# Eight modulation tiles summed on VectorE in the first feed-forward part, gate rows in memory of their own, first loads in four pieces, a seventh tile buffer

## The chip, the cores and the metric

The kernel runs on one core of a Trainium2 chip. The metric is the device time of one execution in microseconds. Before the change, three runs took 2201.83, 2201.08 and 2201.52 us, a median of 2201.52.

## What is computed

Two transformer blocks on 256 tokens of width 1024, batch 1, all in float32. The first block has a mixer (gated convolution, short convolution, windowed pooling), a cross-attention to a memory of 256 tokens, and a mixture of 32 experts of which each token takes four. The second block has two layers, and this is where the change is:

```python
def ada_mod(c, w, b):                      # c: (1, 1024), w: (1024, 6144)
    m = jax.nn.silu(c) @ w + b
    return jnp.split(m[:, None, :], 6, axis=-1)

for layer in range(2):
    shift_m, scale_m, gate_m, shift_f, scale_f, gate_f = ada_mod(c, ada_w[layer], ada_b[layer])
    h = rms_norm(x, norm_gains[layer, 0]) * (1 + scale_m) + shift_m
    y = attention(h) if layer == 0 else retention(h)      # "attn_hybrid_mixer", "retention_mixer"
    x = x + gate_m * y
    h = rms_norm(x, norm_gains[layer, 1]) * (1 + scale_f) + shift_f
    x = x + gate_f * swiglu(h, ffn_w_gate_up[layer], ffn_w_down[layer])
```

The attention of layer 0 has eight heads of stick-breaking attention and eight of causal softmax attention. ada_w holds 2 x 6 x 1024 columns, which the kernel reads as 24 tiles of 1024 x 512.

## The kernel before

**Tiles and units.** All weights pass through a ring of four buffers (`RING = 4`, 2 MB each: 128 partitions, 8 chunks of rows, 512 columns). A planner (class `Plan`) numbers the tiles in the order of their loads; tile n goes to buffer (n + shift) mod 4, and SyncE issues its load in that order once tile n - 4 is freed (`load_tile`; the wait is on the counter in `freed`: finished TensorE products, or finished ada products). SyncE's queue is strictly in order, so a tile whose buffer is not free holds back all behind it.

**Products.** A tile is cut into two units. For each unit ScalarE makes a rounded copy, `w_high` (three buffers, line 1370), and VectorE writes the remainder over the tile itself, `ring_low` (line 1901). TensorE then does three matmuls for each pair of chunks (high x high, high x low, low x high): `feature` (line 753) with the weights as the stationary side, 48 matmuls a unit, or `token` (line 774) with the activations as the stationary side, 24 a unit. `high_until(n)` and `low_until(n)` are the places in ScalarE's and VectorE's program up to which units are prepared; `ahead(g)` is how far before the evacuation of group g.

**Experts.** The 32 experts (and more rounds if an expert has over 64 tokens) run in a loop with six buffers, the four of the ring for the gate-up weights (four tiles of 2 MB, `gu_tile`) and two more for the down weights (`down_tile`). TensorE frees a buffer through `m_tile`. In a round it does gate-up tiles 0 and 1, gathers the next expert's tokens (line 967), gate-up tiles 2 and 3, turns inputs, then the down product (line 1014) and the scatter (line 1039). Behind the experts, the plan's tiles N1, N1 + 1, ... go into the ring again, the first four as soon as the last experts' tiles are used; two of those buffers hold the last expert's down weights until then.

**Modulation.** `ada_product(i)` (line 821) multiplies silu(c) with one ada_w tile on TensorE, eight matmuls with 32 stationary columns, four at a time in different column groups, into a bank that gathers a set of tiles. `ada_take` (ScalarE, line 1503) copies the bank, `ada_reduce` (TensorE, line 829) adds and transposes it, and VectorE adds the bias (`ada_in`, `modulation`). The sets are tiles 0 to 11, 12 to 14, 15 to 21, 22 and 23. Products 12 and 13 stand around the first transposition behind the experts, 14 between `aq[0]` and `ak[0]`, 15 to 21 between the softmax steps of the attention, 22 and 23 at the entry of the first feed-forward part. Their tiles stand at the same places in the order of loads.

**Gates.** For x + gate * y the gate is needed as a row on all partitions: VectorE scales the identity by the gate column (`gate_diags`, line 2500), TensorE multiplies it with ones (`gate_rows`, line 799, banks 4 and 5), ScalarE copies it (`gate_row_in`, line 1465). `gate_diag` and `gate_row` lie in the part of the arena that also holds the softmax pairs, and in layer 0 the three steps stand directly before the product with att_w_o (`ao`).

**Softmax half.** For head pairs m = 0 to 3: `soft_scores` (TensorE, line 1181), `soft_mask` (VectorE, lines 2434 to 2439), `soft_exp` (ScalarE, 1737), `soft_scale` (VectorE, 2449), `soft_turn` (TensorE, 1193), `soft_turned` (ScalarE, 1746), `soft_out` (TensorE, 1109). The pairs are held in two buffers, and the steps of the four pairs interleave in an order written out by hand on each engine.

**Start.** SyncE loads xT in two halves, then the first tile in two column parts, then the parameters, then the rest. ScalarE splits x and the first units, VectorE makes the low parts; its wait for the parameters (`par_in`) stands ahead of the first low part (line 1893).

## Time and profile before

| | |
|---|---|
| median of three runs | 2201.52 us |
| the profiled execution | 2200.33 us |
| its span, first to last instruction | 2198.5 us |
| busy TensorE, weight loads | 2061.8 us (94%), 1380.7 us (63%) |
| busy VectorE, ScalarE | 1027.5 us (47%), 677.4 us (31%) |
| bytes moved | 652.76 MB, 297 GB/s on average |
| chain that ended last | TensorE 61%, DMA 32%, VectorE 4%, ScalarE 2% |

A page of the profile gives sums over the whole span; the stages differ, so the windows, the chain of waits and the timeline are read stage by stage. PE is TensorE, DVE VectorE, ACT ScalarE, SPq the queue of SyncE. The stages lie as follows in the span: start and mixer to about 360 us, cross-attention and routing to 467, experts to 1395, norm and the first transpositions to 1418, attention to 1575 with the softmax half from 1511 to 1552, first feed-forward part from 1587 to 1775, retention to 1997, second feed-forward part to the end.

### The profile page before, as it was taken

Reading aid. Unit: us, or ns where it says so; the run is one execution under the profiler, and the core shown is the slowest. Engines: PE = TensorE matmul, PEld = TensorE weight load, DVE = VectorE, ACT = ScalarE, POOL = GpSimd, SP = SyncE. Lnnn points to the kernel's source line nnn. Section 1 sums busy time; section 2 is a strip of 40 time slices with the busy share of each in tenths; the row PEclk is TensorE's granted clock in tenths of the full one; section 3 lists DMA queues with packets and bytes.
Section 4 is the critical chain, followed back from the end, with each engine's and each line's share of the span. In section 5 each row is a group of like instructions: output and inputs, shape, how many; then the busy total and the mean of one; then the engine's idle time right before and its main releaser. Section 6 shows DMA issues by size and latency. Waiting matters only on the chain.

```text
span 2198.5 us, 30034 instructions
## 1 busy us (share of the span) xinstructions
PE 2061.8 (94%) x12342; PEld 1380.7 (63%) x12342; DVE 1027.5 (47%) x1601; ACT 677.4 (31%) x868; POOL 3.0 (0%) x10
## 2 busy tenths in 40 slices
PE   7999999999999999999999999699899999999998
PEld 7999987743333333333333333485699888878996
DVE  6999857442222222222222223565555556555554
ACT  4343544421111111111111111353533443544333
POOL 0000000000000000000000000000000000000000
PEclk9999999999999999999999999899899999999999
DMA  9555669689999999999999999766845454444552
GB/s 321 183 176 180 239 227 338 233 351 428 428 429 429 427 429 429 428 429 429 428 429 429 428 429 429 289 230 225 273 154 192 172 179 166 154 154 153 175 178 80
DMA packets 182072, 652.76 MB, mean 297 GB/s; under 512 B 6720, under 2 KB 70208, under 8 KB 156896
## 3 DMA queue, kind: packets, MB, share of 16 engines
q1 hardware_dynamic: 181984, 651.47, 75.7%
q8 instruction: 69, 1.13, 0.2%
q14 instruction: 19, 0.16, 0.0%
HBM read 650.40 MB, written 1.05 MB: 296 GB/s over the span
## 4 chain that ended last, share of the span: by engine, by line
PE 61%; DMA 32%; DVE 4%; ACT 2%; issue 1%; SPq 0%; DVEq 0%; ACTq 0%
PE bank L753 31%; DMA ring<-w_down 29%; PE bank L774 13%; PE pair L1014 6%; PE bank L987 4%; DMA ring<-att_w_qkv 1%; DMA ring<-att_w_o 1%; PE pair L821 1%; DVE ring_low L1901 1%; PE bank L742 1%; PE pair L967 1%; ACT arena L1439 1%; DMA par<-params 0%; PE pair L1039 0%; ACT w_high L1370 0%
## 5 line engine op out<-in xcount | busy, mean ns | idle before, releaser
L1901 DVE TENSOR_TENSOR ring_low<-ring,w_high 128x2048 fp32r<-128x2048 f32 (+1 forms) x179 | 404.6, 2266 | 285.0 <-ACT w_high L1370 283.5
L753 PE MATMUL bank<-x_high,w_high 128*128 128x256 f32 x1760 | 502.4, 285 | 17.1 <-DVE ring_low L1893 15.0
L753 PE MATMUL bank<-x_low,w_high 128*128 128x256 f32 x1760 | 499.0, 284 | 0.0
L753 PE MATMUL bank<-x_high,ring_low 128*128 128x256 f32 x1760 | 498.9, 283 | 0.0
L987 PE MATMUL bank<-ring,arena 128*64 128x512 f32 x2048 | 457.3, 595 | 16.6 <-DMA ring<-w_gu 14.8
L1370 ACT ACTIVATE w_high<-ring 128x2048 fp32r<-128x2048 f32 (+1 forms) x179 | 337.7, 1891 | 255.6 <-PE bank L753 122.0
L753 PEld LDWEIGHTS bank<-x_high,w_high 128*128 128x128 f32 x1760 | 338.8, 192 | 21.3 <-issue 20.4
L987 PEld LDWEIGHTS bank<-ring,arena 128*64 128x64 f32 x2048 | 142.0, 137 | 321.6 <-issue 269.6
L753 PEld LDWEIGHTS bank<-x_low,w_high 128*128 128x128 f32 x1760 | 338.9, 193 | 1.1 <-issue 1.0
L2313 DVE TENSOR_TENSOR arena<-bank,par 128x512 f32<-128x512 f32 x64 | 44.0, 687 | 630.8 <-PE bank L997 630.8
L753 PEld LDWEIGHTS bank<-x_high,ring_low 128*128 128x128 f32 x1760 | 338.7, 192 | 0.0
L1014 PE MATMUL pair<-ring,arena 128*64 128x512 f32 x992 | 225.4, 598 | 41.6 <-DMA ring<-w_down 41.6
L774 PE MATMUL bank<-w_high,arena_r 128*128 128x512 f32 x672 | 210.2, 392 | 6.8 <-issue 4.9
L1014 PEld LDWEIGHTS pair<-ring,arena 128*64 128x64 f32 x992 | 67.9, 136 | 178.0 <-issue 177.9
L774 PEld LDWEIGHTS bank<-w_high,arena_r 128*128 128x128 f32 x672 | 127.0, 189 | 37.7 <-issue 8.0
L774 PE MATMUL bank<-ring_low,arena_r 128*128 128x512 f32 x336 | 131.5, 391 | 0.0
L1638 ACT ACTIVATE arena<-bank 128x512 f32<-128x512 f32 x64 | 34.7, 594 | 224.7 <-PE bank L987 224.7
L1950 DVE SCALAR_TENSOR_TENSOR arena<-a_pad,par,arena 128x256 f32<-128x256 f32 x240 | 98.4, 480 | 0.3
L1653 ACT ACTIVATE arena<-pair 128x512 f32<-128x512 f32 x31 | 18.5, 597 | 231.0 <-PE pair L1014 231.0
L1627 ACT ACTIVATE arena<-pair 128x512 f32<-128x512 f32 x32 | 19.1, 597 | 225.5 <-PE pair L967 225.5
L2331 DVE TENSOR_TENSOR arena<-arena,pair 128x512 f32<-128x512 f32 x124 | 76.7, 680 | 5.5 <-PE pair L1039 5.5
L774 PEld LDWEIGHTS bank<-ring_low,arena_r 128*128 128x128 f32 x336 | 63.4, 189 | 13.0
(325 smaller groups left out, 1774.7 us busy)
## 6 DMA issues: line engine op xcount, KB each, us to landing
ring<-w_gu SPq DMA_DIRECT2D x128, 2048.0 KB, 24.9
ring<-w_down SPq DMA_DIRECT2D x63, 2048.0 KB, 25.4
ring<-ada_w SPq DMA_DIRECT2D x24, 2048.0 KB, 11.8
ring<-ffn_w_gate_up SPq DMA_DIRECT2D x44, 1024.0 KB, 7.6
ring<-ret_w_in SPq DMA_DIRECT2D x12, 2048.0 KB, 7.8
ring<-w_in SPq DMA_DIRECT2D x10, 2048.0 KB, 8.1
ring<-w_in SPq DMA_DIRECT2D x16, 1024.0 KB, 10.7
ring<-ffn_w_down SPq DMA_DIRECT2D x8, 2048.0 KB, 7.7
```

What stands on the lines that cost most here:

```text
L742: pe.matmul(acc_bank[:, 0:T], w[:, k, 0:P], xs[:, k, :], start=k + n == 0 and arrival == "x_high", stop=k == b.kc - 1 and arrival == "x_sp ...
L753: mm = pe.matmul(acc_bank[:, ch * T:(ch + 1) * T], w[:, k, ch * P:(ch + 1) * P], xs[:, kk, :], start=kk + ch + n == 0, stop=kk == b.kc - 1 ...
L774: mm = pe.matmul(acc_bank[:, :], xs[:, kk, i * P:(i + 1) * P], w[:, k, :], start=kk + n == 0, stop=kk == b.kc - 1 and n == 2)
L821: mm = pe.matmul(ada_bank[s][o:o + 32, :], silu_c[:, at_col:at_col + 32], at(ada[i])[:, k, :], start=j == 0 and k < 4, stop=last and k >= ...
L987: mm = pe.matmul(bank[b][64 * o:64 * o + 64, :], xgT[:, k // 4, k % 4, :], gu_ring[t][:, j, D * o + 512 * b:D * o + 512 * b + 512], start= ...
L1014: mm = pe.matmul(bank[7][64 * o:64 * o + 64, :], actT[:, k, :], down_ring[t][:, j, 512 * o:512 * o + 512], start=k == 0, stop=k == DC - 1)
L1370: nc.scalar.activation(high_part(u), raw_part(u), ACT.Copy).then_inc(sem("w_high"), 1)
L1638: nc.scalar.activation(gu_s[b], bank[b][:, :], ACT.Copy).then_inc(sem("m_gus"), 1)
L1901: V.tensor_tensor(low_part(u), raw_part(u), high_part(u).bitcast(F32), ALU.subtract).then_inc(sem("w_low"), 1)
L1950: V.scalar_tensor_tensor(out=conv[:, c, :], in0=a_pad[:, c, tap:tap + T], scalar=pc("conv_a_w", tap * DC + c), in1=conv[:, c, :], op0=ALU. ...
L2313: V.tensor_tensor(tv, bank[2 + b][:, :].rearrange("p (c j) -> p c j", c=8), bias, ALU.add).then_inc(sem("m_vec"), 1)
L2331: V.tensor_tensor(acc[:, i, f], acc[:, i, f], bank[4 + q][:, :], ALU.add).then_inc(sem("m_acc"), 1)
```

## The change

- **Start.** The loads of xT and of the first column part of the first tile alternate in halves of 512 KB each; ScalarE and VectorE split them in that order, and VectorE's wait for the parameters moves behind the first low parts. ScalarE does one small activation ahead of the first data.
- **Seventh buffer.** `spare` (16 KB on each partition) takes gate-up tile 0 of expert 1, loaded behind xo[0]. TensorE reads it there in the first round, which is now written out ahead of the loop. The buffer of that tile takes expert 2's instead. The DMA scratch is cut to 512 to make room.
- **Gates.** After that, half of the same memory holds `gate_row` and `gate_diag`. The gate rows of layer 0 are made between `aq[0]` and `ak[0]`, in banks 4 and 6; those of layer 1's retention get their diagonals earlier.
- **Modulation.** The sets are tiles 0 to 11, 12 to 15, 16 to 23. Tiles 12 to 15 are loaded in twos ahead of aq[0] and ak[0] and multiplied around the first transpositions. Tiles 16 to 23 are loaded in the first feed-forward part, and VectorE sums each in eight steps (chunk times a column of silu(c), added up) into 512 columns; TensorE then adds the partitions with a column of ones, four tiles at a time (`ada_rows`). A tile's buffer is freed by its eighth step.
- **Norm.** `mean_w` goes; `ones` takes its place and 1/D moves into the instructions that read the sums.

```diff
-ADA_SETS = (range(0, 12), range(12, 15), range(15, 22), range(22, 24))
+ADA_SETS = (range(0, 12), range(12, 16), range(16, 24))
+ADA_SUMS = len(ADA_SETS[2])
+ADA_AT = (1, 3, 5, 7, 9)
+ADA_STEPS_DOWN = (4, 0, 4, 4, 0, 0)
...
+        spare = sb("spare", [P, 2, 2 * D])
...
+                if i < ADA_SETS[2].start:
+                    t.freed = [("ada_product", i + 1)]
+                else:
+                    t.freed = [("ada_sum", DC * (i - ADA_SETS[2].start + 1))]
...
-        ada_tiles(1)
+        ada_tiles(2)
         aq.append(plan.block([(qkv_w, 0, 512)]))
-        ada_tiles(1)
+        ada_tiles(2)
         ak.append(plan.block([(qkv_w, D, 512)]))
-        ada_tiles(1)
...
-        ada_tiles(len(ADA_SETS[2]))
-        ada_group = plan_groups(1)[0]
         b_outs = plan_groups(2)
         ao = [plan.block([(a["att_w_o_2"][0], 512 * i, 512)], token=True) for i in range(2)]
-        ada_tiles(len(ADA_SETS[3]))
...
             for i in range(FC // 2):
+                if layer == 0 and i in ADA_AT:
+                    ada_tiles(1)
                 gate_up[layer].append(plan.block([(w, 256 * i, 256), (w, FF + 256 * i, 256)]))
...
+            for k in range(2):
+                sp.dma_start(xT[:, chunks_k, :], ...).then_inc(sem(f"x_in{k}"), 16)
+                sp.dma_start(ring[plan.tiles[0].slot][:, chunks_k, first_col:first_col + HALF], ...)
...
                 load_tile(t)
+                if t.n == xo[0].units[0].tile.n:
+                    sp.dma_start(spare[:, :, :], gu_rows(1, 0)).then_inc(sem("spare_in"), 16)
...
             for k, slot in enumerate(first_slots):
                 sp.wait_ge(m_tile[slot], 1)
-                gu_tile(1, k, slot)
+                gu_tile(1 if k else 2, k, slot)
+            for k, slot in list(enumerate(first_slots))[1:]:
+                sp.wait_ge(m_tile[slot], 2)
+                gu_tile(2, k, slot)
...
+            def ada_rows(h):
+                pe.wait_ge(sem("ada_sum"), 4 * DC * (h + 1))
+                for q in range(4):
+                    at_col = ADA_SUMS - 1 - (4 * h + q)
+                    mm = pe.matmul(ada_bank[2][32 * q:32 * q + 32, :], ones_at[:, at_col:at_col + 32], ada_sums[:, q, :],
+                                   start=h == 0, stop=last, skip_group_check=True)
...
-            ada_product(12)
-            turn(t_h[0], lambda: ada_product(13))
+            for i in range(12, 15):
+                ada_product(i)
+            turn(t_h[0], lambda: ada_product(15))
...
             feature(aq[0], s_h[0], turned="h0")
-            ada_product(14)
+            gate_rows(0)
...
-            ada_product(15)
             soft_scores(0)
-            ada_product(16)
             soft_scores(1)
-            ada_product(17)
-            ada_product(18)
             soft_turn(0)
...
-            ada_reduce(2)
-            gate_rows(0)
             split_ready("attn2")
...
-                    ada_product(22)
-                    turn(t_h[1], lambda: ada_product(23))
...
+                    if layer == 0 and i == 7:
+                        ada_rows(0)
...
             token(rv[0], s_h[2])
+            ada_reduce(2)
             token(rv[1], s_h[2])
+            pe.wait_ge(sem("ada_in"), 2)
...
+            def ada_sum(n):
+                for _ in range(n):
+                    m, k = ada_steps[0] // DC, ada_steps[0] % DC
+                    t = ada[ADA_SETS[2].start + m]
+                    dst, w = ada_sums[:, m % 4, :], at(t)[:, k, :]
+                    c = silu_c[:, 32 * k + ADA_WIDTH - 1:32 * k + ADA_WIDTH]
+                    if k == 0:
+                        dve.wait_ge(loaded[t.slot], t.loaded)
+                        if m >= 4:
+                            dve.wait_ge(sem("ada_row"), m // 4)
+                        V.tensor_scalar(dst, w, c, None, ALU.mult).then_inc(sem("ada_sum"), 1)
+                    else:
+                        dve.wait_ge(sem("ada_sum"), ada_steps[0])
+                        V.scalar_tensor_tensor(out=dst, in0=w, scalar=c, in1=dst, op0=ALU.mult,
+                                               op1=ALU.add).then_inc(sem("ada_sum"), 1)
...
                 for i, b in enumerate(gate_up[layer]):
                     g = b.groups[1]
+                    if layer == 0 and i:
+                        ada_sum(4)
                     low_until(ahead(g))
...
+                    if layer == i == 0:
+                        ada_sum(4)
                 if layer == 0:
-                    modulation(1)
+                    for n, steps_n in zip(units_of(down[0][0]), ADA_STEPS_DOWN):
+                        low_until(n)
+                        ada_sum(steps_n)
...
             low_until(units_of(rq[0])[1])
+            ada_sum(8)
...
             low_until(units_of(rv[2])[1])
+            modulation(2)
+            gate_diags(2, 1, 2, None)
```

## Rows read from the trace of the kernel before

**Rows 1.** Windows: stretch, us, busy PE PEld DVE ACT POOL, granted clock, DMA, GB/s.
```profile
617.60:1372.00 754.40, 698.00 (x3239) 248.21 (x3238) 192.28 (x470) 98.28 (x203) 0.00 (x0) 1.00 1.01 428
...
1587.50:1775.00 187.50, 187.50 (x1325) 176.54 (x1326) 101.53 (x86) 75.42 (x58) 0.00 (x0) 1.00 0.55 184
```

**Rows 2.** Timeline of the start: start us, us, engine, line, operation, idle before.
```profile
7.64 2.00 ACT L1380 ACTIVATE x_high<-arena 128x1024 fp32r<-128x1024 f32 x2
...
13.67 1.23 DVE L1893 TENSOR_TENSOR ring_low<-ring,w_high 128x1024 fp32r<-128x1024 f32 x1 [2.58 <-DMA par<-params]
...
15.04 0.55 PE L753 MATMUL bank<-x_high,w_high 128*128 128x256 f32 x1 [15.04 <-DVE ring_low L1893]
...
19.69 1.92 ACT L1370 ACTIVATE w_high<-ring 128x2048 fp32r<-128x2048 f32 x1 [3.98 <-DMA ring<-w_in]
...
29.07 1.92 ACT L1370 ACTIVATE w_high<-ring 128x2048 fp32r<-128x2048 f32 x1 [3.18 <-PE bank L753]
```

**Rows 3.** Stage windows again, one microsecond in the first expert rounds.
```profile
493.00:494.00 1.00, 1.00 (x8) 0.34 (x6) 0.04 (x1) 0.00 (x0) 0.00 (x0) 1.00 0.55 213
```

**Rows 4.** Chain of waits, expert rounds: start us, us, what.
```profile
487.48 7.09 PE bank L987 x32
```

**Rows 5.** Timeline, DMA issues and ScalarE behind the experts.
```profile
1385.59 5.22 SPq L626 DMA_DIRECT2D ring<-ada_w  x1
...
1400.24 1.91 ACT L1370 ACTIVATE w_high<-ring 128x2048 fp32r<-128x2048 f32 x1 [8.54 <-DMA ring<-att_w_qkv]
```

**Rows 6.** DMA issues between 1372 and 1390: count, size, us to landing.
```profile
ring<-ada_w SPq DMA_DIRECT2D x1, 2048.0 KB, 20.0
```

**Rows 7.** Timeline of the softmax half of the attention.
```profile
1513.72 0.42 DVE L2434 COPY arena<-pair 128x256 f32<-128x256 f32 x1 [5.04 <-PE pair L1181]
...
1516.03 0.40 ACT L1737 ACTIVATE arena<-arena,small 128x128 f32<-128x128 f32 x1 [4.50 <-DVE small L2439]
...
1517.70 0.19 ACT L1737 ACTIVATION_READ_ACCUMULATOR arena<-arena,small 128x1 f32 x1
...
1518.75 1.03 DVE L2449 TENSOR_TENSOR arena<-arena,small 128x256 f32<-128x256 f32 x2
...
1521.08 0.87 PE L1193 MATMUL pair<-c,arena 128*128 128x128 f32 x6
...
1535.76 1.92 PE L821 MATMUL bank<-ring,silu_c 128*32 128x512 f32 x16
...
1538.52 0.81 ACT L1746 ACTIVATE cv_pad<-pair 128x768 f32<-128x768 f32 x1 [2.04 <-PE pair L1193]
...
1541.65 1.91 ACT L1370 ACTIVATE w_high<-ring 128x2048 fp32r<-128x2048 f32 x1 [2.32 <-DMA ring<-att_w_o]
...
1547.99 3.78 PE L799 MATMUL pair<-arena,ones 128*128 128x512 f32 x4 [2.02 <-DVE arena L2500]
```

**Rows 8.** Chain of waits, from the attention to the retention part.
```profile
1551.77 11.35 PE bank L774 x48
...
1587.47 3.11 PE bank L742 x24
...
1613.23 103.77 PE bank L753 x864
...
1785.19 3.11 PE bank L742 x24
```

**Rows 9.** Stage windows again, five microseconds of that half.
```profile
1525.00:1530.00 5.00, 5.00 (x34) 2.30 (x28) 1.24 (x4) 2.67 (x9) 0.00 (x0) 0.66 1.05 386
```

**Rows 10.** Timeline of VectorE at two gated additions.
```profile
1575.37 0.68 DVE L2512 TENSOR_TENSOR arena<-bank,arena 128x512 f32<-128x512 f32 x1
...
1774.87 0.69 DVE L2512 TENSOR_TENSOR arena<-bank,arena 128x512 f32<-128x512 f32 x1 [1.82 <-PE bank L774]
```

**Rows 11.** Groups by line, VectorE: count, busy us, mean ns, idle before.
```profile
L2559 DVE SCALAR_TENSOR_TENSOR arena<-arena,small 128x512 f32<-128x512 f32 x4 | 2.8, 749 | 0.1
```

**Rows 12.** Timeline of VectorE at the head of the retention part.
```profile
1786.29 4.49 DVE L1901 TENSOR_TENSOR ring_low<-ring,w_high 128x2048 fp32r<-128x2048 f32 x2
```

More of the change, by code:

```diff
@@ L124, in stop, with block @@
         self.stops.append(len(self.units) - 1)
-    def block(self, parts, rows=D, token=False):
+    def block(self, parts, rows=D, token=False, before_last=None):
         b = Block()
@@ L139, in block @@
                 at += n
+            if before_last and k1 == rows:
+                before_last()
             t = self.tile(cut)
@@ L1285, in _ @@
                 feature(b, s_h[2], turned="h2" if b is rq[0] else None)
+            ada_rows(1)
             def ret_scores(h):
@@ L1505, in _ @@
             act.wait_ge(sem("consts_set"), 3)
-            act.wait_ge(sem("x_in"), 32)
-            split_high("x")
+            nc.scalar.activation(warm, eps[:, 0:1], ACT.Copy)
+            first = plan.units[0]
+            for k in range(2):
+                act.wait_ge(sem(f"x_in{k}"), 16)
+                split_high("x", which=(k,))
+                act.wait_ge(sem(f"first_cols{k}"), 16)
+                nc.scalar.activation(high_part(first)[:, 4 * k:4 * k + 4, :], raw_part(first)[:, 4 * k:4 * k + 4, :],
+                                     ACT.Copy).then_inc(sem("w_high" if k else "first_high"), 1)
+            highs[0] += 1
             high_until(1)
```

207 lines of the change are left out of this document (111 added, 96 removed).

## The prediction

> **What bounds the kernel now.** I read the stage windows first, then the chain of waits stage by stage, then the timeline of single engines wherever the chain leaves TensorE. Two regimes show. In the expert part the DMA share is 1.01 at 428 GB/s and TensorE has 698 of 754 us, so the weight stream is the bound; in the first feed-forward part TensorE is busy 187.50 of 187.50 us while VectorE has 101.5 us of work and the DMA share is 0.55 [rows 1]. What can be won lies between such stretches, where TensorE waits: at the start, at the head of the attention part, in its softmax half, and on entering the feed-forward part. In the softmax half it is a transfer again: ScalarE waits for att_w_o at 1541.65, which sits in the queue behind seven ada_w tiles [rows 7].
>
> **The change part by part.**
>
> *First loads.* TensorE starts at 15.04 after VectorE's first low half at 13.67, and that one waited for the parameters, not for weights [rows 2]. With x and the first columns in alternating halves and the parameter wait moved behind them, the first low half needs half of x_high (1.0 us), half of w_high (1.0) and a low (1.23). Even if nothing starts before 7.64, where x_high starts now, TensorE begins by 10.9; the first two units take it 14.0 us (15.04 to 29.07) and the third unit can't be ready before 19.69 + 1.92 + 2.29 = 23.9, because its tile lands at 19.69 as before (as many bytes ahead of it) [rows 2]. So the third unit starts at 23.9 to 24.9 in place of 29.07: a gain of 4.1 to 5.1, I take **-5.0** (ScalarE's function table is loaded ahead of the data in the new order, which makes the early end likelier). TensorE is full afterwards, so it stays.
>
> *Seventh tile (spare).* The first gate-up tile of expert 1 is loaded early, and the stream is one tile shorter. A tile takes 2.1 MB / 428 GB/s = 4.9 us [rows 1]. But the stream only counts from the moment it no longer waits for slots: at 493 to 494 the DMA share is 0.55, a gap, because the next tile had to wait until TensorE released a slot [rows 3]. TensorE consumes two tiles in 7.09 us, so the next slot is free 3.5 us later [rows 4]. The stream without its first tile restarts 3.5 us later; 4.9 - 3.5 = 1.4 is left, and the tile behind it, whose slot comes two steps later (gather lies between), leaves 1.1. I take **-1.1**, bounds -4.9 (if the gap didn't move) and 0.
>
> *Order of the tiles behind the experts.* Today aq0 is the second tile behind the experts, and ScalarE waits for it in order at 1400.24 (8.54 us idle), ahead of the roots on which all of the token norm hangs [rows 5]. In the new order two ada_w tiles come first and aq0 takes the place of the third: issued at 1385.59, landing 20.0 us later at 1405.6 [rows 5, 6]. That is **+5.4** on the chain; bounds 0 (if the queue were empty) and 5.5. A fourth ada_w tile lands another place behind, before the second transposition needs it, as all of that has moved too. One ada product becomes the gate-row matmuls of layer 0 between aq0 and ak0: about even, and ScalarE's copies of it fit beside ak0's matmuls. In the norm, mean_w becomes ones with the 1/D put into instructions that exist: nothing.
>
> *Softmax half of the attention.* Removed: seven ada products of 1.92, their transfers, the reduce, and the gate-row matmuls (3.78, from 1547.99) in front of att_w_o's product [rows 7]. What remains is the chain of four head pairs. From its rows: mask and maxima from 1513.72 to 1516.03, 2.3; exponentials to 1517.89, 1.9; scaling 1.03 and some 0.2 for the reciprocal ahead of it; transposition 0.87; copy 0.81 [rows 7]. I laid these out in program order from 1510.8, when TensorE leaves the value product: masks 0 and 1 end at 1516.2, turns 0 and 1 start at 1517.5 and 1522.7, mask 2 ends at 1521.4 and mask 3 at 1527.7, exponentials 3 at 1529.5, turn 3 starts at 1530.9, its copy ends at 1532.6. Today that copy ends at 1539.33, so 6.7. Then w_high 1.91 and low 2.29, and att_w_o's product starts at 1536.9 in place of 1551.77 [rows 7, 8]: a gain of 14.9 if TensorE stays at full clock. It won't quite: the granted clock in 1525 to 1530 was 0.66, a mix of its two levels 1.2 and 2.4 GHz, with the products still filling the gaps [rows 9]. Without them TensorE has about 11 us of work in 26, by my layout. Of that 6.1 us lie on the chain; at the low level for all of it they cost 6.1 more, I take half, 3.0. And the next stretch starts cold: at the kernel's start 96 matmuls took 14.0 us, while nine blocks of 96 take 103.77, or 11.53 each, so a cold start costs 2.5; I take 1.8 here [rows 2, 8]. Result **-10.1**, bounds -14.9 and -6.3.
>
> The Trainium skill speaks against the removal here: TensorE: Matmul & The Clock Gate, section on HAM oscillation, says that idle gaps between bursts put TensorE back to the half clock and that a loop can pay this each time. The trace agrees so far as the 0.66 goes. By that rule all the matmuls of this half run at half clock; the first rival below gives the time.
>
> *Entry of the feed-forward part.* From the start of att_w_o's product to the first gate-up matmul it is 35.7 us now (1551.77 to 1587.47) [rows 8]. Now ffn tile 0 is queued behind two ada_w tiles, VectorE starts the last gated addition only at 1575.37, and a product (23) lies between the two transpositions. The entry of the retention part shows the same steps without these: 1774.87 to 1785.19, 10.3 us from the gated addition, against 12.1 here [rows 8, 10]. New: two products of 11.35, the first token group done a quarter of one (2.8) before their end, then 10.3, in all 30.2. Gain 5.5; possibly cold again (0 to 2.5), I take 0.4: **-5.1**, bounds -3.0 and -5.5.
>
> *Feed-forward part 1.* 56 of the 64 summing steps are put here. The nearest row is the 128x512 scalar_tensor_tensor of L2559, 0.749 us [rows 11]; 56 make 42 us, VectorE goes from 101.5 to 143.5 of 187.5 us, so it stays hidden behind TensorE [rows 1]. The order matters more: the steps stand ahead of the low halves that the next block needs. A block is 11.53 us long [rows 8], four steps 3.0; the low half of the next block's first unit ends some 3 us later than now, but it is still needed only at the block's end. Block 1 gets eight steps (6 us), its low ends about 1 us before it is due. Transfers: two gate-up tiles and one ada_w tile in two blocks, about 17 us of 23; a gate-up tile now waits for a slot until the sums have read it, and lands up to 4.5 us into the block before its use, 2.5 us or more in time. If that cover is gone, it costs the overrun of each block. The reduce moves to the retention part at equal price; two ada_rows of four matmuls each are new, half of a product's 1.92 each [rows 7]: **+1.9**.
>
> *Retention part.* Eight steps (6.0) are put between the two low halves at 1786.29 (4.49 the pair) [rows 12]: the second one then ends at 1796.8, and TensorE asks for it 11.5 after 1785.19, at 1796.7: **+0.2**, up to 1. The gate diagonals moved ahead lie beside matmuls. TensorE's wait for the layer-1 columns ahead of the scores comes after two value products: VectorE then needs only its low half, 2.3, and 0.4.
>
> Sum: -5.0 - 1.1 + 5.4 - 10.1 - 5.1 + 1.9 + 0.2 = **-13.8**. The profiled run took 2200.33 (span 2198.5 and 1.8 around it): 2186.5. The median of the three runs is 1.2 above it, 2201.5, so **2187.7**.
>
> **The rivals.**
> *All cold* (the half clock for the whole softmax half and both entries): -6.3 there, -3.0 at the entry in place of -15.2, 5.9 less gain: 2193.6. For it: 0.66 with more work than there will be [rows 9]. Against it: products filled only part of it. Chance 0.15.
> *All warm*: softmax -14.9, entry -5.5, so 5.2 more: 2182.5. 0.14.
> *The spare counts in full* (the gap doesn't move): 3.8 more: 2183.9. The slot release speaks against it. 0.05.
> *VectorE becomes the bound* of the first feed-forward part: it has 86 us free for 56 steps, so from 1.54 us a step it sets the pace [rows 1]; every step also waits for the one before. At 1.9 us: 56 x 0.36 = 20 us more, 2207.9, slower than before. The row of 0.749 speaks against it. 0.05.
> *It doesn't do what it says*: the softmax chain is bound by other waits, and the ordering cost is doubled because products 13 to 15 now precede the transpositions: 0 in place of -10.1 gives 2197.8. 0.07.
>
> **How the numbers follow.** The forecast has 0.54: it covers 2184 to 2191. The range takes in the two clock cases and the full spare, 2180.5 to 2196; left out are the last two rivals and a remainder. A measurement here can tell 0.2%, 4.4 us, from no change: faster means below 2197.1. Forecast, clock cases and spare lie there (0.88), and of the rest a little; the case at 2197.8 is within 0.2%. Faster 0.87, same 0.07, slower 0.06.
>
> **What would show it.** First matmul near 9 and the third unit at 24; a longer gap near 493 and the expert part's end only about 1 us nearer to its start; ScalarE's first w_high behind the experts 5.4 us later in relation to them; no transfer named in the softmax half, att_w_o's product some 28 to 31 us after the value product ends; TensorE still without gaps in the first feed-forward part, VectorE busy near 0.77. It is wrong if summing steps take well over 0.75 us, if TensorE waits for VectorE or for ffn tiles there, or if the experts end 5 us earlier.

## The result, and the profile after

The changed kernel takes 2186.5 us (median of 5 runs, 2186.18 to 2192.34); the kernel before took 2201.52 beside it. The ratio is 0.9942, 95% interval 0.9928 to 0.9957: about 13 us faster, 9 to 16. The profiled execution took 2186.48, span 2184.4, so against the profiled one of before (2200.33) it is 13.85 us; all differences below are between these two unless a line says otherwise.

The page of the changed kernel, its head; VectorE, which had 1027.5 us in 1601 instructions before, has 64 instructions and 44 us more, TensorE (2061.8) 13 us less:

```profile
span 2184.4 us, 29811 instructions
PE 2048.9 (94%) x12222; PEld 1378.0 (63%) x12222; DVE 1071.7 (49%) x1665; ACT 677.3 (31%) x868; POOL 3.0 (0%) x10
```

Stage windows, columns as in [rows 1]. The expert part is the same stage with the same bound; in the first feed-forward part VectorE rises from 101.53 us [rows 1] to 138.72 and TensorE still has no gap; the last three windows lie in and behind the softmax half, where the granted clock is between 0.50 and 0.85:

```profile
611.00:1365.00 754.00, 699.08 (x3246) 248.62 (x3240) 192.25 (x470) 98.42 (x203) 0.00 (x0) 1.00 1.01 428
1568.90:1756.00 187.10, 187.04 (x1315) 175.54 (x1316) 138.72 (x137) 72.95 (x56) 0.00 (x0) 0.99 0.72 247
...
1515.00:1520.00 5.00, 2.31 (x12) 1.25 (x10) 2.98 (x8) 1.73 (x6) 0.00 (x0) 0.50 0.01 2
1520.00:1525.00 5.00, 4.18 (x22) 2.87 (x22) 0.76 (x2) 2.33 (x9) 0.00 (x0) 0.52 0.00 0
1535.00:1540.00 5.00, 2.33 (x7) 1.95 (x8) 4.76 (x3) 4.92 (x5) 0.00 (x0) 0.85 0.00 0
```

Timeline of the start, and of the head of the attention part. The first matmul is at 8.91 in place of 15.04 [rows 2]. VectorE makes the low part of the third unit from 21.79 to 24.08, and TensorE starts on that unit behind it, where it did so at 29.07 before [rows 2]. Behind the experts ScalarE now waits 14.09 us for aq0's tile where it waited 8.54 [rows 5], and TensorE waits 8.93 us for the third modulation tile:

```profile
7.54 1.23 DVE L2088 TENSOR_TENSOR ring_low<-ring,w_high 128x1024 fp32r<-128x1024 f32 x1 [0.24 <-ACT w_high L1555]
8.91 0.55 PE L790 MATMUL bank<-x_high,w_high 128*128 128x256 f32 x1 [8.91 <-DVE ring_low L2088]
21.79 2.29 DVE L1940 TENSOR_TENSOR ring_low<-ring,w_high 128x2048 fp32r<-128x2048 f32 x1 [5.09 <-ACT w_high L1410]
...
1398.90 1.91 ACT L1410 ACTIVATE w_high<-ring 128x2048 fp32r<-128x2048 f32 x1 [14.09 <-DMA ring<-att_w_qkv]
1404.30 3.64 PE L858 MATMUL pair<-ring,silu_c 128*32 128x512 f32 x16 [8.93 <-DMA ring<-ada_w]
```

The chain of waits from the high part of att_w_o's first unit, behind the last softmax head, to the retention part (start us, us, what). No transfer is in it. att_w_o's product starts at 1537.67 (1551.77 before), the first gate-up block at 1568.96 (1587.47), its first 24 matmuls take 4.60 in place of 3.11 [rows 8], and the ten blocks behind it are as dense as before except for 0.99 where `ada_rows(0)` stands (at 1664.54):

```profile
1533.30 1.91 ACT w_high L1410
...
1535.23 2.30 DVE ring_low L1940
...
1537.67 20.94 PE bank L811 x84
...
1568.96 4.60 PE bank L779 x24
...
1583.91 80.63 PE bank L790 x672
...
1768.48 3.10 PE bank L779 x24
```

Groups by line, VectorE, 1568 to 1756 (count, busy us, mean ns, idle before): the summing step costs what L2559's row said, 0.749 [rows 11], and the first step of a tile less.

```profile
L2472 DVE SCALAR_TENSOR_TENSOR spare<-ring,silu_c,spare 128x512 f32<-128x512 f32 x49 | 36.8, 751 | 1.5
L2469 DVE TENSOR_SCALAR spare<-ring,silu_c 128x512 f32<-128x512 f32 x7 | 3.4, 481 | 0.8 <-DMA ring<-ada_w 0.8
```

Read as a ledger, at the same event of both traces (after minus before, and the step since the last line). The feature product of aq0 is the first product of att_w_qkv (queries, first half), the value products are av[0] and av[1] of the same weight:

| event | before | after | offset | step |
|---|---|---|---|---|
| second expert's rows gathered (PE) | 494.39 | 489.23 | -5.2 | -5.2 |
| last expert's last scatter | 1391.80 | 1384.92 | -6.9 | -1.7 |
| aq0's feature product starts | 1418.56 | 1417.22 | -1.3 | +5.5 |
| second value product ends | 1510.91 | 1507.74 | -3.2 | -1.8 |
| att_w_o's product starts | 1551.77 | 1537.67 | -14.1 | -10.9 |
| block 0 of the first feed-forward part, 24 matmuls in | 1590.58 | 1573.56 | -17.0 | -2.9 |
| retention part entered | 1785.19 | 1768.48 | -16.7 | +0.3 |
| its second value half (x24) | 1872.13 | 1857.52 | -14.6 | +2.1 |
| span | 2198.5 | 2184.4 | -14.1 | +0.5 |

### The profile page after: what moved, and what is told of

It reads as the page before. It is cut to its first block, busy times and chain, and to the rows that moved or that the text cites. A ratio compares the mean times of both kernels' runs of the same rounds, so it can differ in the third digit from the quotient of the medians.

```text
span 2184.4 us, 29811 instructions
## 1 busy us (share of the span) xinstructions
PE 2048.9 (94%) x12222; PEld 1378.0 (63%) x12222; DVE 1071.7 (49%) x1665; ACT 677.3 (31%) x868; POOL 3.0 (0%) x10
## 4 chain that ended last, share of the span: by engine, by line
PE 60%; DMA 32%; DVE 4%; ACT 2%; issue 1%; SPq 0%; DVEq 0%; ACTq 0%
PE bank L790 30%; DMA ring<-w_down 30%; PE bank L811 14%; PE pair L1068 6%; PE bank L1040 4%; DMA ring<-att_w_qkv 1%; DVE ring_low L1940 1%; PE bank L779 1%; DMA ring<-w_in 1%; ACT arena L1479 1%; PE pair L1015 1%; PE pair L858 1%; PE pair L1093 0%; ACT w_high L1410 0%; PE bank L976 0%
```

## The experiments

Twelve kernels were run, each beside the kernel before on the same chip. Since the changed kernel's ratio is 0.9942, an experiment's ratio minus 0.9942, times 2201.5, is its distance from it; the intervals are some 3 us wide on each side, so where a verdict is finer than that it rests on the traces, from event to event.

### start_alone: the first loads alone, in the kernel before

```diff
-            sp.dma_start(xT[:, 0:4, :], ...).then_inc(sem("x_in"), 16)
-            sp.dma_start(xT[:, 4:8, :], ...).then_inc(sem("x_in"), 16)
+            for k in range(2):   # half k of x, then half k of the first columns
+                sp.dma_start(xT[:, chunks_k, :], ...).then_inc(sem(f"x_in{k}"), 16)
+                sp.dma_start(ring[...][:, chunks_k, first_col:first_col + HALF], ...).then_inc(sem(f"first_cols{k}"), 16)
```

> The kernel before with the first loads of the new kernel alone (four pieces, ScalarE's table loaded early, the parameter wait moved behind the first low halves). My theory: first matmul near 9 us in place of 15.04, third unit near 24.1 in place of 29.07, and these 4.6 to 5.0 us stay to the end: 2201.5 - 4.8 = 2196.7. Rival: the stream of the expert part takes them back, because its transfers were issued by slots that come free earlier but the stream is the bound: then the expert part ends less than 1 us earlier and the total is 2200.5 to 2201.5.

Measured: first matmul at 8.70; median 2197.37 of 11 runs against 2201.97 of 23, ratio 0.9978 (0.9969 to 0.9987), that is 4.8 us, 3 to 7. The theory holds, the rival falls. The profiled execution alone would have misled: it took 2201.75, the highest of the eleven, and the gain was gone in it by 487 us. Where it went stands in the last section.

### order_alone: the order of the tiles alone, in the kernel before

```diff
-        ada_tiles(1)
+        ada_tiles(2)
         aq.append(plan.block([(qkv_w, 0, 512)]))
...
         ak.append(plan.block([(qkv_w, D, 512)]))
-        ada_tiles(1)
```

> The kernel before with one edit: the second modulation tile behind the experts goes ahead of aq0, which becomes the third tile. My theory (ScalarE waits in order for aq0, ahead of the roots): ScalarE's first w_high behind the experts starts 4.9 to 5.6 us later (1405 to 1406), everything behind it too: 2201.5 + 5.4 = 2206.9. Rival: what counts is the landing of the last modulation tile ahead of the transpositions; then this order costs nothing (0 to 1 us), because here only two modulation products precede the second transposition, as before.

Measured: 2205.55, ratio 1.0017 (1.0008 to 1.0026), 3.7 us slower (1.8 to 5.7). ScalarE's timeline:

```profile
1409.72 1.91 ACT L1369 ACTIVATE w_high<-ring 128x2048 fp32r<-128x2048 f32 x1 [14.15 <-DMA ring<-att_w_qkv]
```

From the last scatter (1395.66) to this it is 14.06, in the kernel before 8.44 (1391.80 to 1400.24 [rows 5]), and to the feature product 32.37 against 26.76: +5.6. It is the changed kernel's own number (32.30). The price at its place is as forecast. The trace keeps it to the end: the feed-forward part is entered at 1596.89 against 1587.47, 9.4 later, of which 3.95 are there at the second expert's gather, ahead of the edit (the router's stage), and 5.5 come from the edit. The median's smaller number has 5.6 within its interval. The rival (no cost) falls.

### no_spare: the changed kernel without the early tile

```diff
-                if t.n == xo[0].units[0].tile.n:
-                    sp.dma_start(spare[:, :, :], gu_rows(1, 0)).then_inc(sem("spare_in"), 16)
```

(and the expert loops start at 0 again, with the tile in the stream)

> The changed kernel without the early load of expert 1's first gate-up tile (the memory stays, for the gate rows). My theory: the early tile is worth 1.1 (forecast) to 1.8 us (read from the trace), as the gap of the stream near 490 us becomes shorter again when the tile is in the stream: 2186.5 + 1.8 = 2188.3. Rival: it counts in full, a tile's 4.9 us: 2191.4. Second rival: worth nothing, 2186.5.

Measured: 2191.25, ratio 0.9958 (0.9945 to 0.9970), 3.5 us slower than the changed kernel, with an interval of about 4 on each side: by the times no verdict. In the traces the stretch from the second gather to the last scatter takes 896.64 without the early tile and 895.64 to 896.22 in eight kernels that have it (the changed one 895.69; in a ninth 897.10); the stretch ahead of it takes 27.05 from the first expert's product, against 26.84. So the tile is worth about 1 us, not 4.9. The kernels built on the one before take 897.2 to 897.7 there; of the 1.7 us of the ledger some 0.8 are thus not the tile's, and what they are was not tried.

The gap of the stream is where the forecast put it. One-microsecond windows of the changed kernel; DMA share and GB/s are the last two columns, and [rows 3] is the one of before with 0.55:

```profile
488.00:489.00 1.00, 1.00 (x8) 0.46 (x6) 0.09 (x1) 0.00 (x0) 0.00 (x0) 1.00 0.04 16
489.00:490.00 1.00, 1.00 (x6) 0.35 (x4) 0.00 (x0) 0.00 (x0) 0.00 (x0) 1.00 0.00 0
```

### roots_first: ScalarE's roots ahead of aq0

```diff
-            high_until(units_of(aq[0])[0])
             for i in range(TT):
                 root(i, 0)
                 sum_squares(i)
                 rms_root(i, True)
+            high_until(units_of(aq[0])[0])
```

> The changed kernel with one edit: ScalarE takes the roots and the squares of the token norm first and the first half of aq0 (whose transfer it waits for 14 us) behind them. My theory of the forecast (only ScalarE's in-order wait costs): the roots no longer wait, the feature product of aq0 starts 5 us or more earlier, about 2181. Rival: TensorE is held by the landing of the third modulation tile too (its product starts at 1404.30 ahead of the transpositions): then the gain is 0 to 1 us and the time is 2185.5 to 2186.5.

Measured: 2187.64, ratio 0.9933 (0.9920 to 0.9946), 2 us better, 0 not excluded. From the last scatter to the feature product 31.34 in place of 32.30: 1 us. TensorE's timeline names the second chain, which the forecast did not have:

```profile
1405.99 3.64 PE L858 MATMUL pair<-ring,silu_c 128*32 128x512 f32 x16 [8.92 <-DMA ring<-ada_w]
```

The rival holds: two engines wait, in order, for two tiles, and to take one wait away brings only what the other leaves. The Trainium skill, TensorE: Matmul & The Clock Gate, section on the array's architecture, calls the queues of ScalarE and VectorE strictly first in, first out; the 14.09 us in which ScalarE had the roots to do and did not agree.

### head_reordered: both waits taken away

```diff
-            for i in range(12, 15):
-                ada_product(i)
-            turn(t_h[0], lambda: ada_product(15))
+            ada_product(12)
+            turn(t_h[0], lambda: ada_product(13))
...
             gate_rows(0)
+            ada_product(14)
+            ada_product(15)
```

(with roots_first's edit, and ak0's tile ahead of the tiles 14 and 15)

> The edit of roots_first, and with it the modulation products 14 and 15 moved behind aq0's feature product and the gate rows, their tiles behind ak0's tile (aq0 stays the third tile). My theory: the head of the attention part is held by two chains, ScalarE's in-order wait for aq0 and TensorE's in-order wait for the third modulation tile; with both gone the roots start where VectorE's aggregation ends (1389.0) and not at 1400.7, so aq0's feature product starts 10 to 11 us earlier (about 1406.5 in place of 1417.2); two products of 1.9 now lie between aq0 and ak0 where they were ahead of it, so 3.8 of it is not paid twice. Time 2186.5 - 10 = 2176.5. Rival A: the landing of aq0 (1398.9) and its high and low parts hold the start, then -6: 2180.5. Rival B: the tiles behind it (att_w_qkv, in the same queue) land too late for the next blocks and TensorE waits there: 0 to -3, 2183.5 to 2186.5.

Measured: 2187.54, ratio 0.9937 (0.9924 to 0.9949): 1 us. The first step came as expected: the feature product starts at 1408.88, 23.37 behind the last scatter in place of 32.30. Then it is gone by the end of the second value product (122.48 behind the last scatter, 122.82 in the changed kernel). The chain and ScalarE's timeline say where:

```profile
1423.61 3.57 PE pair L858 x32
...
1459.85 3.44 issue
```
```profile
1447.88 1.91 ACT L1411 ACTIVATE w_high<-ring 128x2048 fp32r<-128x2048 f32 x1 [5.71 <-DMA ring<-att_w_qkv]
```

The two products, which lay in the wait before, are now in series (3.6). aq1's tile has moved into the slot that ak0's tile holds, so its transfer could only start when ak0 was done (1439.75), and ScalarE waits for it in order until 1447.88, ahead of the exponentials on which VectorE's chain for the second scores hangs. That chain starts 75.0 behind the last scatter (1460.51), in the changed kernel 75.3 (1460.25), although the first value product ended 4 us earlier; TensorE waits 3.44 for it. The matmuls of aq0 started at the lower clock as well (24 in 4.38, 3.11 in the changed kernel). 8.9 - 3.6 - 3.4 - 1.3 = 0.6, and 0.3 was measured. Rival B holds for the 3.4, by a slot; the other 4.9 are the products in series and the clock.

### ro_gate_rows_first

```diff
+            gate_rows(2)
             token(ro[0], ret_split, ("ret_split", 0, 4))
-            gate_rows(2)
             token(ro[1], ret_split, ("ret_split", 0, 4))
```

> The changed kernel with one edit: the gate-row matmuls of the retention part go ahead of ro[0]'s product instead of between ro[0] and ro[1]. ScalarE takes the gate rows in order ahead of the high part of ro[1]'s first unit, so that unit's halves (1.9 and 2.3 us) can only be made after ro[0] has ended, and TensorE waits 4.86 us at 1949. Theory: that stall goes, 2186.5 - 4.9 = 2181.6. Rival: the halves of ro[1] are late by its transfer, then no change, 2186.5.

Measured: 2182.36, ratio 0.9914 (0.9900 to 0.9928): 6 us better. The chain of the changed kernel, and of this one:

```profile
1925.68 21.80 PE bank L811 x96
1947.47 1.72 PE pair L836 x4
1949.19 4.86 issue
1954.05 21.34 PE bank L811 x84
```
```profile
1927.91 1.72 PE pair L836 x4
1929.63 40.86 PE bank L811 x180
```

49.7 us become 42.6. 4.86 is the pause; the other 2.2 is what the same 84 matmuls cost more behind a pause (21.34, against 40.86 - 21.80 = 19.06). The eight kernels here that have the pause took 20.90 to 21.83 for these 84, so the second part is there each time. A stall costs itself and the clock behind it.

### fill_softmax: matmuls without a purpose in the gaps of the softmax half

```diff
+            def filler():
+                for _ in range(2):
+                    mm = pe.matmul(bank[fill_group % BANKS][:, :], ones[:, :], c1[:, 0:512], start=True, stop=True)
+                mm.then_inc(sem("filler"), 1)
...
+            filler()
             soft_scores(1)
+            filler()
             soft_turn(0)
```

> The changed kernel with six groups of two matmuls (128x128 by 128x512, 0.85 us each at full clock) put back into the gaps of the softmax half, with no transfer behind them. Theory (the clock): the granted clock there rises from 0.5-0.85 towards 1.00, the turns of the heads take 0.87 instead of 1.54 us, att_w_o's product is entered and the feed-forward part is entered (first 24 matmuls 3.11 in place of 4.60) at full clock: 3 to 5 us less, 2182.5. Rival: the fillers lie on the chain themselves (each is in order ahead of a score or a turn) and give back as much: 0 to +3 us, 2186.5 to 2189.5.

Measured: 2189.35, ratio 0.9941 (0.9929 to 0.9954): no difference. The windows of this kernel:

```profile
1525.00:1530.00 5.00, 3.76 (x22) 1.71 (x20) 3.00 (x8) 1.62 (x6) 0.00 (x0) 1.00 0.00 0
1535.00:1540.00 5.00, 1.57 (x15) 0.96 (x12) 2.71 (x2) 4.92 (x5) 0.00 (x0) 0.81 0.00 0
1540.00:1545.00 5.00, 5.00 (x13) 3.86 (x13) 5.00 (x3) 2.48 (x2) 0.00 (x0) 0.51 0.02 3
```

The fillers did what they should: granted clock 1.00 through the half, turns of 0.87 us in place of 1.54, and from the first turn to the last copy 16.4 us (1519.06 to 1535.45) in place of 19.0 (1514.36 to 1533.40), 2.7 less. But in these 16.4 a group of fillers stands on the chain itself, ahead of the last turn:

```profile
1532.04 1.91 PE bank L1303 x4
1533.95 0.67 PE pair L1251 x6
```

So the lower clock costs 2.7 + 1.9 = 4.6 us there. The chain says the same piece by piece: TensorE's turns, scores and head outputs on it from the first turn on take 11.2 us in the changed kernel and 6.7 in this one. Of the 4.6 the fillers gave back 1.9 here and 2.2 ahead of the first turn, where three groups of them stand (8.9 us behind the value product in place of 6.6). Then the clock fell again in the pause between the last head and att_w_o's product, whose 84 matmuls took 21.76, 0.8 more than in the changed kernel. The rival holds: the gain was given back. Whether fillers that never stand on the chain would keep some of the 4.6 was not tried.

### sums_doubled: each summing step twice in blocks 1 to 10

```diff
+                        if twice:
+                            V.scalar_tensor_tensor(out=dst, in0=dst, scalar=1.0, in1=dst, op0=ALU.mult,
+                                                   op1=ALU.max).then_inc(sem("ada_again"), 1)
+                            dve.wait_ge(sem("ada_again"), again[0])
```

> The changed kernel with every summing step behind the first of a tile in the ten gate-up blocks 1 to 10 of the first feed-forward part done with one more VectorE step of the same form and shape (maximum of the sum with itself, 0.75 us, and a wait for it), 35 more steps, about 28 us of VectorE. Per block VectorE has 2 x 2.3 (low parts), 0.75 + 0.4 + 0.5 (hidden) and 4 x 0.75 = 9.2 of 11.5 us now, 12 with the doubling. Theory (VectorE hidden until its work per block passes TensorE's 11.5): the part gets 0.5 us longer per block, 5 us in all, 3 to 9: 2191.5. Rival (the order matters before the sum: the low parts behind the sums arrive late as soon as the slack of 1 us is gone): 10 us or more, 2196.5 or above. Third: the slack is larger than I think, then no change.

Measured: 2191.87, ratio 0.9954 (0.9940 to 0.9967). The same stretch, block 0's last 72 matmuls to the block behind `ada_rows(0)`, in the changed kernel and in this one:

```profile
1573.56:1665.53 91.97, 91.97 (x757) 90.04 (x756) 72.30 (x73) 33.70 (x25) 0.00 (x0) 1.00 0.75 250
```
```profile
1577.46:1670.49 93.03, 92.58 (x757) 90.21 (x756) 86.60 (x96) 33.36 (x25) 0.00 (x0) 1.00 0.70 234
```

1.06 us longer with VectorE busy 0.93 of the time: by the price the third outcome. The added step takes 0.69, not 0.75, and there are 25 in this stretch (the first step of a tile has none), 17.3 us. But VectorE is no longer hidden. In the changed kernel the chain stays on TensorE from 1583.91 to 1664.54; here it runs over the steps and the low parts behind them from 1586 to 1646 (and over one gate-up transfer of 9.02, into a buffer that the sums free), and TensorE is idle for 0.45 us:

```profile
1594.62 0.76 DVE spare L2479
1595.41 0.70 DVE spare L2476
...
1596.89 2.50 DVE ring_low L1940 x2
1599.38 1.82 issue
```

So the load is just at the point from which VectorE sets the pace, and the price there is still small. (Its profiled execution also has 3.4 us more by the second gather, 492.58, ahead of everything that the edit touches.) This also puts that point where it belongs: in the changed kernel a block leaves 11.5 - 9.0 = 2.5 us free beside its four steps, so it is 1.3 to 1.4 us a step, not the 1.54 that the whole part's average gave. The doubled steps bear it out: a tile's eight take 7 x 1.51 + 0.43 = 11.0 us in this chain, 1.4 each.

### no_products_before: the removed products without their work, in the kernel before

```diff
+                if i in ADA_SETS[2]:   # tiles 15 to 21: wait for the tile, one narrow matmul
+                    arrived(ada[i])
+                    mm = pe.matmul(ada_bank[2][0:32, 0:64], silu_c[:, 0:32], at(ada[i])[:, 0, 0:64], ...)
+                    mm.then_inc(sem("ada_product"), 1)
```

> The kernel before, where the seven modulation products of the softmax half (15 to 21) do almost no matrix work: one matmul of 64 columns each in place of 16 of 512 (four of 512 for the first), at the same places, with the same waits for their tiles; so the layer-1 modulation is computed from part of its sums. The transfers and the releases of their slots stay. Theory (the transfers are the price, att_w_o lands last in the queue): att_w_o's product starts at most 2 us earlier than 1551.77, 2200 to 2202. Rival (the products themselves fill TensorE's gaps and sit on the chain): they are 13.4 us, most of the 14.1 that the change gained up to there goes with them, 2190.

Measured: 2202.67 against 2201.39, ratio 1.0006 (0.9997 to 1.0015). The chain of this kernel:

```profile
1512.07 9.13 DMA ring<-ada_w
1521.20 20.73 DMA ring<-att_w_o
...
1541.96 1.92 ACT w_high L1378
...
1548.29 3.78 PE pair L799 x4
1552.07 8.15 PE bank L774 x34
```

Some 12 us of TensorE's work are gone and att_w_o's product starts where it did (1551.77 [rows 8]). The products themselves were free; the queue of tiles ahead of att_w_o held ScalarE's first high part of it. But this kernel keeps the reduce and the gate rows, and they stand behind that transfer, so the run does not make the queue the whole price. In the kernel before the reduce ran at this place:

```profile
1544.10 1.87 PE L829 MATMUL bank<-rows,c 128*128 128x7 f32 x8 [3.84 <-ACT c L1503]
```

From the end of the value product to that high part it is 30.7 us before (1510.91 to 1541.65 [rows 7]) and 25.6 in the changed kernel (1507.74 to 1533.30): 5.2 of the 10.9. From there to att_w_o's product it is 10.1 before, with ScalarE's copy of the bank, the reduce, the diagonals and the gate rows (3.78), and 4.4 after, with none of them: 5.7. The queue was thus about half of what the change took from the path in this half, and the reduce and the gate rows the other half.

### early_high: att_w_o's first high part two heads earlier

```diff
             soft_turned(1)
+            high_until(units_of(ao[0])[0])
             soft_exp(3)
             ...
             soft_turned(3)
-            high_until(units_of(ao[0])[0])
```

> The changed kernel with one edit: ScalarE makes the high part of att_w_o's first unit two heads earlier, behind the copy of head pair 1 (it idles 4.4 us there) and not behind that of pair 3, so VectorE can make the low part right after the last scaling (1530.7) and TensorE does not wait 3.34 us at 1537.67. Theory: att_w_o's product starts at 1534.2, 3.4 us earlier, and the shorter pause leaves TensorE's clock higher by up to 1.1 us: 2186.5 - 3.4 to 4.5 = 2182.5. Rival: the second half of the attention output (copy, high, low) is late next, and TensorE waits for it in the middle of the first unit instead: -1, 2185.5.

Measured: 2184.38, ratio 0.9920 (0.9907 to 0.9934): 5 us better. att_w_o's product starts 27.4 behind the value product's end in place of 29.9, its first 84 matmuls end 47.3 behind it in place of 50.9, and block 0 has its first 24 matmuls done 60.8 behind it in place of 65.8: 2.6, then 3.5, then 5.0. The pause is shorter by 2.6, and 0.9 comes back by the clock in the product: 1.00 where the changed kernel had 0.81. The last 1.5 (3.11 for block 0's 24 matmuls in place of 4.60) is not shown to be the edit's: of the six other kernels with the changed kernel's code there, five took 4.59 to 4.60 and head_reordered took 3.11. The rival's mechanism is there too, at a small price: TensorE waits 0.32 at 1544.32 for the low part of the second unit.

```profile
1540.00:1545.00 5.00, 4.68 (x21) 3.59 (x20) 4.25 (x3) 4.65 (x4) 0.00 (x0) 1.00 0.00 0
```

### tiles_late: modulation tiles 12 to 15 into the softmax half

```diff
-        ada_tiles(2)
         aq.append(plan.block([(qkv_w, 0, 512)]))
-        ada_tiles(2)
...
             soft_scores(1)
+            ada_product(12)
+            ada_product(13)
             soft_turn(0)
             soft_scores(2)
+            ada_product(14)
...
             soft_scores(3)
+            ada_product(15)
```

> The changed kernel with the four modulation tiles 12 to 15 taken out of the head of the attention part: aq0 is the first tile behind the experts, ScalarE takes the roots first, and the four products go into the gaps of the softmax half (12 and 13 behind the second score, 14 and 15 behind the third and the fourth), their tiles between the qkv tiles and att_w_o, the reduce behind the last head. Theory: as in head_reordered aq0's feature product starts 8.3 us earlier (1408.9), now without two products (3.6) in series behind it and without aq1's tile in the slot of ak0's, which took the gain there; the fillers showed that products in those gaps cost nothing; the reduce adds 0.8: 2186.5 - 7.5 = 2179.0. Rival A: att_w_o lands late again, as it did before the change (its slots are freed by products 12 and 13 at 1500 to 1503, it lands 7 to 12 us later): the gain is 3 to 5 us smaller. Rival B: VectorE's 16 us chain between av0 and the second scores is the bound of the first half and keeps its place, then the gain is lost there as in head_reordered: 2186.5.

Measured: 2180.93, ratio 0.9904 (0.9889 to 0.9919): 8.4 us better. From the last scatter to the end of the second value product 114.3 in place of 122.8, so the whole gain of the earlier start is kept. In the softmax half a transfer is back in the chain:

```profile
1508.46 14.48 DMA ring<-ada_w
...
1522.98 3.64 PE bank L861 x16
```

It is the last modulation tile's (15); att_w_o's product starts 31.9 behind the value product in place of 29.9. Behind it 0.2 come back in the 84 matmuls (20.71) and 1.5 in block 0's first 24 (3.11), which is again not shown to be the edit's. The theory holds and rival B falls. Of rival A about half of the price is there, 2.0, but by another tile: what lands late is modulation tile 15 and not att_w_o.

### all_three: tiles_late, early_high and ro_gate_rows_first together

> tiles_late, early_high and ro_gate_rows_first in one kernel. If their gains add: 2186.5 - 7.5 - 3.5 - 4.9 = 2170.6. If att_w_o's transfer is late in tiles_late, the early high part gains nothing in it: 2174 to 2177.

Measured: 2169.68 (2168.38 to 2174.50), ratio 0.9862 (0.9845 to 0.9878) to the kernel before. That is within 1 us of the sum that was expected, 2170.6, and the fastest of all. The three measured gains make 19.4 us (8.4, 4.8 and 6.2) and 17.6 are here, so they add within the intervals. The other expectation, that early_high gains nothing beside a late transfer, falls: modulation tile 15 still holds the chain for 14.26 us, but att_w_o's tile is there at 1515.80 and its product starts 28.3 behind the value product, 31.9 in tiles_late. Its chain:

```profile
1529.88 19.18 PE bank L814 x84
...
1916.37 40.86 PE bank L814 x180
```

att_w_o's 84 matmuls take 19.18 (20.94 in the changed kernel), and the retention's output product has no pause.

## Why the prediction was right, and where it was off

The forecast was 2187.7 and 13.8 us of gain; 2186.5 was measured, and 13.85 between the profiled executions. Term by term:

- *First loads*, -5.0 forecast: -4.9 at the third unit (24.1 against 29.07), -4.8 in start_alone. The bound named, the third unit's tile and its halves, was the one that held. The first matmul moved by 6.1 us, of which the parameter wait was 2.58 [rows 2]; no run has the pieces without it or it without the pieces.
- *Seventh tile*, -1.1: about -1 for the tile (no_spare). The reason given, that the gap moves with the slot release, is what the DMA share shows. The stage as a whole gained 1.7; 0.8 of it is not explained.
- *Order of the tiles*, +5.4: +5.5 in the ledger, +5.6 in order_alone. The size was right, the reason only half of it. I put the whole wait on ScalarE; roots_first shows that TensorE's wait for the third modulation tile holds the same point: without ScalarE's wait the feature product starts only 1 us earlier. The sentence that a fourth tile "lands another place behind, before the second transposition needs it" looked at the wrong tile: the third one, ahead of the first transposition, was the one to look at.
- Between the feature product and the second value product 1.8 came in that no term had; 1.5 of it is the clock at aq0's first 24 matmuls (4.60 before, 3.11 after). Kernels with the changed kernel's code up to there show both, 3.11 (sums_doubled) and 4.48 to 4.61 (early_high, fill_softmax, ro_gate_rows_first), so it is no property of the change.
- *Softmax half*, -10.1: -10.9 up to att_w_o's start, and its 84 matmuls cost 1.8 more than at full clock (20.94 against 19.18 in all_three), so -9.1 on the same account. The chain was laid out at 26.1 us at full clock and 29.1 with the clock; 29.9 was measured. The first clock term was mis-sized: 3.0 in the forecast, 4.6 by fill_softmax. The layout without it was 0.7 too long, which hides a part of that. The second, 1.8, measured 1.8. no_products_before shows that the products were free; of what was gained up to att_w_o's start the transfers were about half (5.2) and the reduce and the gate rows behind them the other (5.7). The Trainium skill, TensorE: Matmul & The Clock Gate, section on HAM oscillation, says that gaps between bursts put TensorE back to the half clock. The rows give 0.50 and 0.52 in the middle of the half and 0.81 to 0.85 at its end, with waits of 3.5 us ahead of the first three turns, so the trace agrees on the mechanism. Half clock on all of TensorE's work in the chain had been put at 6.1 (*all cold*); 4.6 is three quarters of it.
- *Entry of the feed-forward part*, -5.1: -2.9 in the ledger, -4.7 when the 1.8 above is counted where it was forecast. The steps that were laid out at 30.2 took 29.5 (31.3 less the 1.8), and the cold start took 1.5 (24 matmuls in 4.60), for which 0.4 had been set aside: this term was mis-sized by 1.1. It is the end of 2.5 that was named as a bound, reached in part; head_reordered, with the same code there, took 3.11 and had none of it.
- *Feed-forward part*, +1.9 and *retention part*, +0.2: +0.3 and +2.1, in sum 2.4. The reduce's removal (0.8) pays for the first `ada_rows` (0.99) in the one part, and both others fall into the next. The steps cost 0.751 against 0.749, TensorE waited for none.

So the mechanisms hold, but that the total came within 1.2 us is in part luck: the unforecast 1.8, most of it a clock that differs between executions of the same code, cancels the softmax half's clock and the entry. Of the rivals, *all cold* is true for three quarters of the softmax half and for a part of the entry, *all warm* for neither, and both fall in sum; *the spare in full* falls by the traces of no_spare (its times alone leave it open); *VectorE the bound* falls, and its point of decision was put too far out by taking the average over the part instead of a block; *it does not do what it says* falls by the chain without a transfer and att_w_o's product 29.9 behind the value product.

## What to carry to other kernels

Where two engines wait in order for two tiles of one queue, take both waits away or none, and then look which slot each following tile has moved into: head_reordered won 8.9 us and gave 3.4 of them back to that, the rest to products in series and the clock. A pause of TensorE costs twice, once itself and once in the matmuls behind it, so cut the pause ahead of a long product (early_high, ro_gate_rows_first). Matmuls that only keep the clock up pay for themselves only where they are not on the chain: fill_softmax won 4.6 us and its own fillers took 4.1 of them. Before the price of a stage is put down to one transfer, read what stands between its landing and the next product: here a second chain of the same size stood there. Work that waits for late tiles was best placed in gaps near to where its result is needed (tiles_late, 8 us), and a bound of an engine's free time is to be taken per block, not per stage.

## What was not expected of the hardware

The stage of the router, between attention and experts, takes a different time in executions of the same code. From the tenth modulation product to the second expert's gather it is 45.55 us in the kernel before (448.84 to 494.39), 45.03 in the changed one, 48.49 in start_alone and 50.02 in order_alone (448.32 to 498.34), although the last two have the code of the kernel before in this stage. Kernels with the changed kernel's code to there spread too, from 45.00 (fill_softmax) to 48.25 (sums_doubled). Windows of before and of order_alone:

```profile
460.00:465.00 5.00, 4.06 (x26) 1.59 (x18) 4.65 (x16) 1.01 (x3) 0.00 (x0) 0.97 1.03 436
```
```profile
460.00:465.00 5.00, 4.86 (x22) 2.69 (x16) 4.14 (x13) 1.06 (x3) 0.00 (x0) 0.50 1.04 439
465.00:470.00 5.00, 3.62 (x12) 1.13 (x10) 2.89 (x20) 1.19 (x2) 0.00 (x0) 0.50 0.94 398
```

TensorE runs small matmuls with short waits between them there, and the clock goes to its lower level and comes back at a moment that differs: both had fallen between 455 and 460 (0.69 and 0.58), one had it back by 465 and the other not before 470. That is up to 4.5 us between executions of the same code, about as much as the largest single edit of this change. It took 2.9 us of start_alone's gain out of its profiled run (3.1 were left at the tenth product, 0.2 at the gather; the other 1.7 had gone ahead of this stage) while the medians showed the gain. It may be what parts the changed kernel's five runs into three at 2186.2 to 2186.5 and two at 2191 and 2192; those were not traced, so that stays open.
